# A two-block decoder kernel whose opening stage, gate weights and first gated-delta head are reordered

## The reference

```python
c_act = silu(c)
mod = c_act @ ada_w[layer] + ada_b[layer]                 # 1024 x 6144, twice
shift_m, scale_m, gate_m, shift_f, scale_f, gate_f = split(mod, 6)
h = rmsnorm(x, norm_mix_g) * (1.0 + scale_m) + shift_m
proj = h @ w_in                                           # 1024 x 4112
qkv, gate, a_in, b_in = proj[:3072], proj[3072:4096], proj[4096:4104], proj[4104:4112]
qkv = silu(causal_depthwise_conv(qkv, conv_w))            # 4 taps
beta = sigmoid(b_in); g = -exp(a_log) * softplus(a_in + dt_bias)
o = chunk_gated_delta_rule(q, k, v, g, beta)              # 8 heads of 128, chunks of 64
x = x + gate_m * (rmsnorm(o) * silu(gate)) @ w_out
x = x + gate_f * swiglu(rmsnorm(x) * (1 + scale_f) + shift_f)
```

## Time and profile before

| | before |
|---|---|
| device time, median of 3 (lowest, highest) | 2285.94 us (2283.67, 2286.65) |
| profiled execution: its device time | 2285.54 us |
| profiled execution: span | 2283.7 us |
| PE busy, share of the span | 2172.8 us, 95% |
| DVE, ACT, POOL busy | 1180.9, 580.8, 1218.6 us |
| mean granted TensorE clock | 0.99 of full speed |

### The profile page before, as it was taken

The page is one execution under the profiler, slowest core; times in us unless marked ns, Lnnn a source line. Parts: engine busy times, 40 slices in busy tenths (PEclk is TensorE's granted clock), DMA queues, the critical chain, the costliest instruction groups (busy, mean ns, idle before and its releaser), DMA issues.

```text
span 2283.7 us, 29290 instructions
## 1 busy us (share of the span) xinstructions
PE 2172.8 (95%) x11996; PEld 1732.7 (76%) x11996; DVE 1180.9 (52%) x1634; ACT 580.8 (25%) x1053; POOL 1218.6 (53%) x690
## 2 busy tenths in 40 slices
PE   5899999889999999998999999999999999999998
PEld 4667777667888887776788888877767778887886
DVE  4556666646737466454522222457766365445333
ACT  3242333313202112343220211332232231002113
POOL 4523333336777777522566666654435266656763
PEclk9999999999999999999999999999999999999999
DMA  8333222215646464210333333322214133333331
GB/s 287 99 102 89 70 84 93 84 41 173 220 138 211 148 202 122 80 50 28 110 102 94 100 95 99 93 83 74 65 49 127 47 96 107 93 93 92 102 102 65
DMA packets 366016, 240.40 MB, mean 105 GB/s; under 512 B 11350, under 2 KB 350524, under 8 KB 365756
## 3 DMA queue, kind: packets, MB, share of 16 engines
q1 hardware_dynamic: 364268, 234.60, 34.2%
q10 hardware_dynamic: 1616, 3.93, 0.5%
HBM read 234.31 MB, written 4.19 MB: 104 GB/s over the span
## 4 chain that ended last, share of the span: by engine, by line
PE 87%; DVE 7%; ACT 3%; issue 2%; DMA 1%; POOL 0%; SPq 0%; ACTq 0%; DVEq 0%; POOLq 0%
PE bank L565 16%; PE bank L567 16%; PE bank L566 16%; PE bank L584 6%; PE bank L586 5%; PE bank L585 5%; PE mid L831 2%; PE mid L1272 1%; PE bank L601 1%; PE bank L603 1%; PE bank L602 1%; PE mid L609 1%; PE bank L800 1%; PE bank L802 1%; PE bank L801 1%
## 5 line engine op out<-in xcount | busy, mean ns | idle before, releaser
L526 POOL TENSOR_SCALAR wH<-stage 128x1024 fp32r<-128x1024 f32 (+1 forms) x342 | 383.2, 1120 | 1009.3 <-PE bank L586 377.0
L528 POOL TENSOR_TENSOR wL<-stage,wH 128x1024 fp32r<-128x1024 f32 (+1 forms) x342 | 836.6, 2446 | 28.6
L565 PE MATMUL bank<-hH,wH 128*128 128x512 f32 x944 | 368.7, 391 | 0.7 <-DVE A L1970 0.3
L567 PE MATMUL bank<-hH,wL 128*128 128x512 f32 x944 | 367.4, 389 | 0.0
L566 PE MATMUL bank<-hL,wH 128*128 128x512 f32 x944 | 367.3, 389 | 0.0
L565 PE MATMUL bank<-RA,wH 128*128 128x512 f32 (+1 forms) x852 | 311.8, 366 | 13.9 <-ACT tb L1412 7.9
L566 PE MATMUL bank<-RA,wH 128*128 128x512 f32 (+1 forms) x852 | 307.9, 361 | 0.0
L567 PE MATMUL bank<-RA,wL 128*128 128x512 f32 (+1 forms) x852 | 307.7, 361 | 0.0
L584 PE MATMUL bank<-hH,wH 128*128 128x512 f32 x544 | 239.3, 440 | 4.7 <-DVE A L2114 4.5
L586 PE MATMUL bank<-hH,wL 128*128 128x512 f32 x544 | 214.2, 394 | 0.0
L585 PE MATMUL bank<-hL,wH 128*128 128x512 f32 x544 | 213.7, 393 | 0.0
(11 more groups left out here) (370 smaller groups left out, 3121.5 us busy)
## 6 DMA issues: line engine op xcount, KB each, us to landing
WIDE<-in_ada_t SPq DMA_DIRECT2D x48, 1024.0 KB, 5.9
stage<-in_ffn_w_gate SPq DMA_DIRECT2D x44, 512.0 KB, 3.8
stage<-in_ffn_w_up SPq DMA_DIRECT2D x44, 512.0 KB, 3.8
stage<-in_c_wkv SPq DMA_DIRECT2D x32, 512.0 KB, 3.9
stage<-in_gdn_w_in SPq DMA_DIRECT2D x32, 512.0 KB, 4.0
stage<-in_ffn_w_down SPq DMA_DIRECT2D x32, 512.0 KB, 3.8
stage<-in_o_w_in SPq DMA_DIRECT2D x32, 512.0 KB, 4.0
stage<-in_e_w_in SPq DMA_DIRECT2D x26, 512.0 KB, 3.7
```

Source lines behind the costliest of these rows:

```text
L526: pool.tensor_scalar(high[:, 0:n], raw[:, 0:n], 1.0, 0.0, ALU.mult, ALU.add).then_inc(w_high, 1)
L528: pool.tensor_tensor(low[:, 0:n], raw[:, 0:n], high[:, 0:n].bitcast(F32), ALU.subtract).then_inc(w_split, 1)
L565: pe.matmul(bank[:, 0:n], h[:, k, c], xh[:, k, :], start=first and k == 0, stop=False)
L567: mm = pe.matmul(bank[:, 0:n], l[:, k, c], xh[:, k, :], start=False, stop=last and k == kc - 1)
```

## The change

- `c`: `silu(c)` is written to `cbc` and then copied to two PSUM banks, `c_bank` (the banks B6 and B5). The eight sums of the beginning read it there; later ones read `cbc`. For that `x_turn` uses B4 and B3, and `rstd` of the first norm lies in SS.
- Order at the beginning: DVE makes `ada_sum(0)` ahead of `memory_low`; SP issues the gate weights and `load_ada(2)` ahead of `x`.
- Gate weights: no slabs of `PLAN` any more, but two loads of 32 KB into `ab_raw`, split once on POOL (`split_gates`, 384 columns) ahead of kv slab 4. PE multiplies them block by block in turn with head slab 0.
- First head: on PE two blocks of slab 1 stand ahead of the gate transposes, and `gate_sums` stands three blocks into slab 2. On DVE `conv(0, 0)` stands between the gates' first copy and the rest, `conv(0, 1)` after `gates`. On ACT the gate arithmetic is mixed with `head_sum(0, 0)` and `(0, 1)`; SiLUs and squares of rows 0 and 1 come ahead of `head_sum(0, 2)`; `head_gate(0)` comes last, ahead of `head_start(0)`.
- Two copies: `kv_copies(0)` moves from `head(7)` into `head_end(6)`, ahead of its wait for `yt_ready`.
- `kv2` and `kv3` are summed in B3 and B7 with a semaphore of their own, `kv_copied`, and no longer use `acc`.

```diff
-PLAN = [("m0", 8), ("ab", 2), ("gdn", 32), ("kv0", 2), ("kv1", 2), ("gdn_out", 8), ("kv2", 2)]
+PLAN = [("m0", 8), ("gdn", 32), ("kv0", 2), ("kv1", 2), ("gdn_out", 8), ("kv2", 2)]
-    _u += {"ab": 0, "mla": 7 * 4}.get(_name, _n)
+    _u += {"mla": 7 * 4, "kv2": 0, "kv3": 0}.get(_name, _n)
+        ab_raw, ab_high, ab_low = A[:, 14, 0:384], RA[:, 0, 0:384], RA[:, 1, 0:384]
+        c_bank, x_banks = mid[:, 3:5].rearrange("p a c -> p (a c)"), (B4, B3)
...
             load_ada(1)
+            for j in range(2):
+                sp.dma_start(ab_raw[:, 192 * j:192 * j + 64].rearrange("p (k c) -> p k c", k=4),
+                             win[512 * j:512 * (j + 1), 4 * D:4 * D + 16].rearrange("(k p) c -> p k c", p=P)).then_inc(g["ab_in"], 16)
+            load_ada(2)
             sp.dma_start(A[:, 0:8].rearrange("p (t a) c -> p t (a c)", t=TT),
...
-            load_ada(2)
             load_kv(2)
...
-            for j in range(2):
-                load(SLAB0["ab"] + j, ...)
...
+            def split_gates():
+                pool.wait_ge(pool_own, 2)
+                pool.wait_ge(g["ab_in"], 32)
+                pool.tensor_scalar(ab_high, ab_raw, 1.0, 0.0, ALU.mult, ALU.add).then_inc(g["ab_hi"], 1)
+                pool.wait_ge(g["ab_hi"], 1)
+                pool.tensor_tensor(ab_low, ab_raw, ab_high.bitcast(F32), ALU.subtract).then_inc(g["ab_lo"], 1)
...
+                    if name == "m0" and i == 4:
+                        split_gates()
...
-            pe.wait_ge(w_split, ab + 2)
+            pe.wait_ge(g["ab_lo"], 1)
             for k in range(KD):
                 pe.wait_ge(h_ready, k + 1)
...
-            mm.then_inc(slab_done, 2)
+                if k == KD - 1:
+                    mm.then_inc(g["ab_ps"], 1)
+                pair_chunks(SLAB0["gdn"], USE0["gdn"] // 2, (k,))
...
-            head_sums(0, range(KD))
+            head_sums(0, range(KD, KD + 2))
             gates_of_tokens()
-            head_sums(0, range(KD, 2 * KD))
+            head_sums(0, range(KD + 2, 2 * KD + 3))
             gate_sums()
-            head_sums(0, range(2 * KD, 4 * KD))
+            head_sums(0, range(2 * KD + 3, 4 * KD))
...
-            kv_slabs("kv2", range(2))
+            def kv_beside(n):
+                if n > 2:
+                    pe.wait_ge(kv_copied, 2 * n - 4)
+                for j in range(2):
+                    s = SLAB0[f"kv{n}"] + j
+                    pe.wait_ge(w_split, s + 1)
+                    product((B3, B7)[j], s, memH, memL, n=MEM).then_inc(slab_done, 1)
+            kv_beside(2)
             ffn(0, 2)
-            kv_slabs("kv3", range(2))
+            kv_beside(3)
...
             act.wait_ge(c_in, 16)
-            act.activation(cbc[:], cbc[:], ACT.Silu).then_inc(m["c"], 1)
+            own(act.activation(cbc[:], cbc[:], ACT.Silu))
+            own.settle()
+            act.activation(c_bank, cbc[:], ACT.Copy).then_inc(m["c"], 1)
...
             def head_end(i):
                 inv_sqrt(g["oss"], i + 1, ors, B4[:], 1.0 / P, load=False).then_inc(g["ors"], 1)
+                if i == 6:
+                    act.wait_ge(g["qn"], 8)
+                    kv_copies(0)
                 act.wait_ge(yt_ready, i + 1)
...
-                    act.wait_ge(g["qn"], 8)
-                    kv_copies(0)
                     kv_copies(1)
...
-            for j in range(3):
-                head_sum(0, j)
...
-            head_gate(0)
             act.preload_act_table_set(SILU)
-            for j in range(3):
+            for j in range(2):
                 head_silu(0, j)
             for j in range(2):
                 head_square(0, j)
+            head_sum(0, 2)
+            head_silu(0, 2)
             act.preload_act_table_set(LN_EXP)
+            head_gate(0)
             head_start(0)
...
-                    ins = dve.tensor_tensor_reduce(out=w, in0=w, in1=cbc[:], scale=1.0, ...
+                    ins = dve.tensor_tensor_reduce(out=w, in0=w, in1=c_bank if n < ADA_HEAD else cbc[:], scale=1.0, ...
...
+            ada_sum(0)
             for n in range(4):
                 memory_low(0, n)
-            for n in range(ADA_HEAD):
+            for n in range(1, ADA_HEAD):
                 ada_sum(n)
```

More of the change, by code:

```diff
@@ L305, in build @@
         g = {n: sem("g_" + n) for n in (
-            "abT", "ab", "gates", "gsum", "pick", "rowsum", "rowhi", "rowlo", "row", "silu", "sq", "ss", "rn", "rows", "kb", "qn", "dec", "erow", "gram", "ktr",
+            "ab_in", "ab_hi", "ab_lo", "ab_ps", "abT", "ab", "gates", "gsum", "pick", "rowsum", "rowhi", "rowlo", "row", "silu", "sq", "ss", "rn", "rows", "kb", "qn", "dec", "erow", "gram", "ktr",
             "vtr", "xt", "x", "xq", "p_ps", "p", "xp", "tok", "v", "wt_ps", "wt", "v_ps", "vn", "s_ps", "s", "o_ps", "osq", "oss",
@@ L716, in x_turn @@
                         pe.wait_ge(x_ready, k - 1)
-                    turn_over((B4, B5)[k % 2], [xtok[:, t, k * P:(k + 1) * P] for t in range(TT)]).then_inc(turned, 1)
+                    turn_over(x_banks[k % 2], [xtok[:, t, k * P:(k + 1) * P] for t in range(TT)]).then_inc(turned, 1)
             def norm_squares(ks):
@@ L1602, in head @@
                 head_end(i)
-            for j in range(3):
-                head_sum(0, j)
+            act.preload_act_table_set(LN_EXP)
+            head_sum(0, 0)
+            ab = B3[:, 0:64].rearrange("p (t h) -> p t h", h=16)
+            act.wait_ge(g["azb"], 1)
+            act.activation(tmp8[:, 0], ab[:, :, 8:16], ACT.Exp, scale=-1.0).then_inc(g["eb"], 1)
+            act.wait_ge(par_in, 64)
+            own(act.activation(bc8[:, 0, :], bc8[:, 0, :], ACT.Exp))
+            act.wait_ge(g["azb"], 1)
+            own(act.activation(tmp8[:, 3], tmp8[:, 2], ACT.Exp, scale=-1.0))
+            own.settle()
+            act.activation(tmp8[:, 3], tmp8[:, 3], ACT.Ln, bias=1.0).then_inc(g["sp"], 1)
+            head_sum(0, 1)
+            act.wait_ge(g["gsum"], 1)
+            gc = B4[:, 0:32].rearrange("p (t h) -> p t h", h=8)
+            act.activation(tmp8[:, 0], gc, ACT.Exp).then_inc(g["gexp"], 1)
+            act.wait_ge(g["zab"], 2)
+            act.activation(tok[:, 3], tok[:, 3], ACT.Exp).then_inc(g["gexp"], 1)
             act.wait_ge(g["rowsum"], 1)
@@ L1910, in product_of @@
                 def product_of(k, j):
-                    dve.scalar_tensor_tensor(out=tn[j][:], in0=xT[:, k, :], scalar=gain[:, k:k + 1], in1=rstd[:],
+                    dve.scalar_tensor_tensor(out=tn[j][:], in0=xT[:, k, :], scalar=gain[:, k:k + 1], in1=SS if which == "mix0" else rstd,
                                              op0=ALU.mult, op1=ALU.mult).then_inc(t_ready, 1)
```

117 lines of the change are left out of this document (52 added, 65 removed).

## The result

| | before | after |
|---|---|---|
| device time, median of 4 (lowest, highest) | 2286.3 us (2283.67, 2286.7) | 2261.8 us (2256.74, 2262.44) |
| profiled execution: span | 2283.7 us | 2260.3 us |
| PE busy | 2172.8 us | 2165.2 us |
| mean granted TensorE clock | 0.99 | 0.993 |

After divided by before is 0.989, 95% interval 0.9873 to 0.9908: 24.5 us faster by the medians, 23.4 by the spans. The forecast was 28.9 us and 2257.0 (2248 to 2266). The sign and the range were right, the size 5 us too hopeful.

A forecast was written before the change was run, and what follows sets the result against it. PE bounds the kernel, with 87% of the span. Beginning through head 0 (18.8 us), head 7 (7.2) and the places behind `kv2` and `kv3` (2.9) sum to 28.9, taking 2285.94 to 2257.0 us; eight-in-ten range 2248 to 2266.

The forecast's parts named there:

- Part 1: Up to the end of kv slab 7: earlier loads start slab 2 1.5 us earlier at full clock; 4.2 us won.
- rival D: Modulation sums: the PSUM read does not free DVE from POOL, sums stay at 1.7 us; 2259 us; chance 0.05.
- Part 2: The norm: head slab 0 runs block by block with the gates' product and hides there; 2.9 us won.
- I let it fall again: In the norm: the clock falls to 1.2 GHz for 3.3 us, costing 1.6; 4.5 us won if it holds.
- Parts 3 and 4: First head: slabs 1 to 3 without late inputs win 9.8 us; squares and rows without idle time win 1.9.
- Part 5: Head 7: `kv_copies(0)` ahead of `yt_ready` removes PE's 7.91 us stand; 7.2 us won (5 to 9.3).
- I let L2138 end at 455.4: Head 7: allowance for L2138 beside POOL's earlier split, putting `out_step` at 458.1; 7.2 us won instead of 9.3.
- rival B: Head 7: two splits hold L2138 and its followers, 3 us won instead of 7.2; 2261 us; chance alone 0.07.
- Part 6: Behind `kv2` and `kv3`: with other banks the pairs' waits of 1.44 and 1.45 us go; 2.9 us won.
- A: Beginning: loads and stages, not PE, set slabs 4 to 7; 24 us won, 2262; chance 0.19 with part of rival B.
- C: More won: clock held in the norm (1.6), full 9.3 in head 7, 1.8 more early; 2251.5 us; chance 0.11.
- E: Modulation sums: the operation on PSUM is slow, 5.0 us a row gives 2290, slower than before; chance 0.01.

The follow-up runs named there:

- late_sum: The changed kernel with before's start order: `ada_sum(0)` behind `memory_low` on VectorE, `load_ada(2)` behind `x` and the small loads on SyncE; 2266.52 us.
- sums_sbuf: The changed kernel with all modulation sums reading row c from SBUF (`cbc`) as before, the copy into PSUM kept; 2265.89 us.
- warm: The changed kernel plus 15 products nobody reads, in PE's two stands of head 7 (2.18 and 1.85 us); 2262.36 us.
- hold: The changed kernel plus one GpSimd wait: the second `gdn_out` slab's split waits for `yt_ready` of head 6; 2260.35 us.
- gates_first: The changed kernel with `conv(0, 0)` behind the gates on VectorE, as before; 2264.26 us.
- kv_acc: The changed kernel with `kv2` and `kv3` multiplied in the two accumulators and copied from there, as before; 2267.26 us.
- filled: The kernel of `hold` plus products nobody reads at seven places where PE stands for 1.7 to 3.8 us; 2252.70 us.
- h7_only: The kernel before with one edit: `kv_copies(0)` ahead of the wait for `yt_ready` in head 7; 2285.76 us, ratio 0.9997.
- before_filled: The kernel before plus products nobody reads where PE stands for over 1.9 us, its waits kept; 2274.70 us.

## Why the prediction was right, and where it wasn't

**Part 1**: 4.2 forecast, 3.8 measured. The wait before slab 2 is 1.20 us (forecast 1.1), the clock held, and SyncE no longer stands for `load_ada(2)`. Right in each step; `late_sum` confirms it, at 2.5 us for the order alone. The prediction called row c from PSUM "off the path" (rival D: 2 us); `sums_sbuf` shows 1.5 us on the path and up to 4 with the clock behind it. The eighth sum ended at 62.8, not near 61: DVE waited 1.76 us for its last load.

**Part 2**: 2.9 forecast, 4.3 measured (8.1 - 3.8). Slab 0 did hide in the norm. "I let it fall again" didn't come: the clock held, and nearly the upper end of 4.5 was reached. That is luck. Behind the same wait of 2.54 or 2.55 us, with the same code up to there, the clock held in after and `warm` and fell in `hold`, `gates_first` and `kv_acc`. After's stretch comes first, then that of `hold`:

```profile
68.00:76.00 8.00, 6.02 (x25) 4.49 (x26) 6.74 (x10) 4.02 (x6) 4.35 (x3) 1.00 0.75 207
...
68.00:76.00 8.00, 6.12 (x20) 4.88 (x21) 6.84 (x10) 4.02 (x6) 4.18 (x3) 0.79 0.76 215
```

**Parts 3 and 4**: 11.7 forecast (9.8 + 1.9), 12.3 measured (20.4 - 8.1). Waits gone as worked out, the squares come with no wait at 100.77 against 102.4 less the 1.0 from part 2.

**Part 5**: 7.2 forecast, 4.1 measured. The step that failed is "I let L2138 end at 455.4". I had the right mechanism from the earlier trace rows and charged it once. But every VectorE operation from L2152 to L2138 lies beside the splits, the 4-column copy too: L2138 ended at 436.3, which is 456.7 in before's time, 1.3 later. And behind it PE stood for 2.18 and 1.85 us, with the lower clock after both, which the sum had not:

```profile
436.69 0.66 PE L846 MATMUL mid<-inv,A 64*64 64x64 f32 x16 [2.18 <-DVE inv L2163]
...
439.19 0.76 PE L815 MATMUL bank<-RA,wH 128*128 128x512 f32 x1 [1.85 <-ACT tb L1437]
```

The first `out_step` at 439.19 is 459.6 in before's time, 1.5 later than forecast; the other 1.6 of the missing 3.1 us went behind it, at the lower clock. That is rival B, at 4.1 instead of its 3.

**Part 6**: 2.9 forecast, 1.2 measured (1.1 by `kv_acc`). "With other banks the wait is gone" named only one of two things the first pair waits for. It also waits for the split of its second slab, which needs the third weight buffer, and that is free only when `kv2`.0 is multiplied. I had not asked who waits for the slab behind.

**Rivals.** A didn't happen in either half. C was half right: the beginning gave 20.4 where C had 20.4 + 1.8, head 7 nothing of it. D and E are refuted by the 1.28 us of the sixteen rows. Together the errors of the parts are +1.6, -3.1 and -1.7, which leaves 25.7; behind `kv3`, a fall of the clock (1.5) and two waits of 0.36 and 0.32 us near the end take it to 23.5, against 23.4 in the spans. The range held in part because errors of opposite sign met: the lucky clock of part 2 is 1.4 of the +1.6.

**The fastest run.** After was once 5.1 us under its median, 2256.74, with a clock of 0.995 instead of 0.992 or 0.993. The 12.0 us of falls in the profile come in pieces of 1.7 us, so three fewer would explain it; that is argued, not shown, since that run has no profile.

## What to carry to other kernels

Where an engine's buffer comes free earlier, look at what it triggers: here an earlier split took back part of what the removed wait gave, and one more wait on GpSimd returned 2.6 us of it. A stand of PE can cost twice, by itself and by the clock behind it; where it can't be removed, products nobody reads fill it (7.7 us from `hold` to `filled`), and with them two kernels can be compared with less of the clock's luck. A wait of 7.91 us removed alone (`h7_only`) showed nothing in the median of ten runs, so look at the place itself and not only at the total. When a wait is removed, list everything the waiting instruction waits for, since the next in line sets the gain.

## What was not expected of the hardware

- Stands of PE of 1.4 to 2.9 us were followed by 1.2 GHz in some executions and not in others, at the same place of the same code: 2.12 us ahead of the latent scores left the clock at 1.00 in before and at 0.59 in after; behind 2.54 us ahead of the norm it stayed at 1.00 in after and was 0.76 and 0.77 from 68 to 72 us in `hold` and `gates_first`. What decides it between executions stays open.
- Executions of one kernel differ mainly by this: before took 2284.0 us at a mean clock of 0.990 and 2290.7 at 0.987. `before_filled` spread over 0.8 us.
- A VectorE copy of 4 columns took 2.36 us instead of 0.16 beside a split on GpSimd.
- An operand in PSUM cost the modulation sum nothing: 1277 ns in the median against 1276 for the shortest from SBUF. The 62 cycles that the prediction cites from the Trainium skill (VectorE: DVE Perf Modes, section on the TRN2 errata) don't show here.
